# An expert loop whose TensorE text is laid out in another order: the 128-wide text moved ahead of the 144- and 160-wide ones

## What is computed

```python
D_MODEL, SEQ, N_EXPERTS, TOP_K, D_FF = 1024, 1024, 32, 4, 1024

top_vals, top_idx = lax.top_k(logits, TOP_K)
gates = jax.nn.softmax(top_vals, axis=-1)
# per expert e, on the tokens xb that chose it:
h = xb @ gu_w[e] + gu_b[e]                      # gu_w[e]: 1024 x 2048
x_glu = jnp.minimum(h[:, 0::2], SWIGLU_LIMIT)
x_lin = jnp.clip(h[:, 1::2], -SWIGLU_LIMIT, SWIGLU_LIMIT)
act = x_glu * jax.nn.sigmoid(SWIGLU_ALPHA * x_glu) * (x_lin + 1.0)
y = act @ dn_w[e] + dn_b[e]                     # dn_w[e]: 1024 x 1024
# y times its gate is added to the token's row
```

## Time and profile before

| | us |
|---|---|
| median of 3 runs | 2246.07 (2245.27 to 2248.84) |
| the profiled execution, own time | 2249.02 |
| its span in the trace | 2247.4 |
| TensorE matmuls busy | 2189.1 (97%) |
| TensorE weight loads busy (beside the matmuls) | 1594.6 (71%) |
| VectorE / ScalarE / GpSimd busy | 1283.0 / 472.6 / 344.5 |

### The profile page before, as it was taken

How to read it: one execution, slowest core, us unless ns; L and a number is a source line. 1 busy time by engine, 2 the same in 40 slices (tenths; PEclk the granted TensorE clock), 3 DMA queues, 4 the chain that set the end, 5 groups by cost and what they waited for, 6 DMA issues and landing times.

```text
span 2247.4 us, 49136 instructions
## 1 busy us (share of the span) xinstructions
PE 2189.1 (97%) x19188; PEld 1594.6 (71%) x19189; DVE 1283.0 (57%) x2529; ACT 472.6 (21%) x975; POOL 344.5 (15%) x356
## 2 busy tenths in 40 slices
PE   8999998899999999999999999999999999999997
PEld 3444444888545777887788877788778887788775
DVE  6566533455565455656555655566655665556664
ACT  3233001444423111111211111111111111111113
POOL 0000001122013212111121211122111221121211
PEclk9999999999999999999999999999999999999998
DMA  3111111332435868988888987799877998679987
GB/s 144 51 60 42 52 66 60 87 105 81 177 132 175 319 257 302 335 307 304 305 301 294 353 301 279 263 336 352 304 285 279 336 352 317 257 293 333 356 303 266
DMA packets 120367, 534.90 MB, mean 238 GB/s; under 512 B 27540, under 2 KB 61480, under 8 KB 87521
## 3 DMA queue, kind: packets, MB, share of 16 engines
q1 hardware_dynamic: 98416, 489.30, 56.5%
q0 software_dynamic: 21904, 44.98, 7.9%
HBM read 484.58 MB, written 40.05 MB: 233 GB/s over the span
## 4 chain that ended last, share of the span: by engine, by line
PE 95%; DMA 1%; issue 1%; DVE 1%; ACT 0%; SPq 0%; POOL 0%; another core or an unknown queue 0%; POOLq 0%; DVEq 0%; ACTq 0%
PE ps L2395 43%; PE ps L2441 17%; PE ps L1831 9%; PE ps L1929 5%; PE ps L2211 3%; PE ps L2425 2%; PE ps L2028 2%; PE ps L2476 2%; PE ps L1878 1%; PE ps L2037 1%; PE ps L2202 1%; PE ps L2010 1%; PE ps L2042 1%; PE ps L2130 1%; DMA arena<-sum_s 1%
## 5 line engine op out<-in xcount | busy, mean ns | idle before, releaser
L2395 PE MATMUL ps<-arena 128*128 128x128 f32 (+2 forms) x8192 | 986.4, 284 | 5.4 <-issue 3.7
L2395 PEld LDWEIGHTS ps<-arena 128*128 128x128 f32 x8192 | 978.2, 191 | 18.1 <-issue 16.1
L2441 PE MATMUL ps<-arena 128*64 128x512 f32 x1984 | 393.4, 543 | 2.4
L1685 DVE TENSOR_TENSOR arena<-arena 128x1024 f32<-128x1024 f32 x248 | 294.3, 1218 | 0.0
L2441 PEld LDWEIGHTS ps<-arena 128*64 128x64 f32 x1984 | 140.4, 137 | 207.2 <-issue 191.9
L1672 DVE TENSOR_SCALAR arena<-ps,arena 128x160 f32<-128x160 f32 x256 | 98.0, 383 | 306.1 <-PE ps L2395 304.0
L1086 ACT ACTIVATE arena<-arena 128x160 f32<-128x160 f32 x256 | 86.1, 336 | 802.9 <-DVE arena L1672 802.9
L1831 PE MATMUL ps<-arena 128*128 128x512 f32 x448 | 195.7, 594 | 0.0
L774 POOL DMA_INDIRECT sum_s<-arena,idx_s x31 | 51.5, 1660 | 841.2 <-ACT arena L1101 841.2
L1831 PEld LDWEIGHTS ps<-arena 128*128 128x128 f32 x448 | 84.7, 190 | 109.2 <-issue 109.2
L1929 PE MATMUL ps<-arena 128*128 128x512 f32 x280 | 120.6, 593 | 0.8 <-ACT arena L914 0.8
(11 more groups left out here) (292 smaller groups left out, 2141.7 us busy)
## 6 DMA issues: line engine op xcount, KB each, us to landing
arena<-gu_w SPq DMA_DIRECT2D x128, 2048.0 KB, 11.7
arena<-dn_w SPq DMA_DIRECT2D x128, 1024.0 KB, 13.9
arena<-dn_b SPq DMA_DIRECT2D x32, 512.0 KB, 15.3
arena<-w_in_t SPq DMA_DIRECT2D x26, 512.0 KB, 3.3
arena<-arena SPq DMA_DIRECT2D x50, 256.0 KB, 2.7
arena<-w_out SPq DMA_DIRECT2D x2, 2048.0 KB, 8.3
arena<-x SPq DMA_DIRECT2D x8, 512.0 KB, 3.5
xn_s<-arena SPq DMA_DIRECT2D x8, 512.0 KB, 2.6
```

The lines of the kernel that those rows point to most:

```text
L1685: nc.vector.tensor_tensor(dst[:, w, :], a[:, w, :], b[:, w, :], op).then_inc(s_ds, 1)
L2395: last = nc.tensor.matmul(ps[:, f % 2, k * C:k * C + size], wslot[u][:, kt, o:o + P], xT[:, kt, 0:size], start=kt == 0, stop=kt == KT - 1, ...
L2441: last = nc.tensor.matmul(ps[rows, bank, 0:width], acts[:, k, :], weights[:, k, :], start=first and k == 0, stop=k == K2 - 1, skip_group_c ...
```

## The change

In `gate_product` the condition is turned round, so that the 128-wide text is built first and the two wider ones with their shared steps second. The steps, their operands, widths and waits stay as they are. A 128-wide expert now runs into its text without a jump and jumps over the others at its end; a wider one jumps over the 128-wide text at its head and runs into the last steps without a jump.

```diff
             def gate_product(need, n, m):
-                with pe.If(need > 1):
+                with pe.If(need < 2):
+                    gate_up(n, m + 1, SIZES[0], range(0, END - SHARED))
+                with pe.Else():
                     with pe.If(need == 2):
                         gate_up(n, m + 1, SIZES[1], range(0, WIDE))
                     with pe.Else():
                         gate_up(n, m + 1, SIZES[2], range(0, WIDE))
                     gate_up(n, m + 1, C, range(WIDE, END - SHARED))
-                with pe.Else():
-                    gate_up(n, m + 1, SIZES[0], range(0, END - SHARED))
                 gate_up(n, m + 1, C, range(END - SHARED, END))
```

## The result

The change made the kernel slower, by very little: 2251.13 us median against 2247.17, 17 runs each, a ratio of 1.0017 with a 95% interval of 1.0010 to 1.0023, that is 2 to 5 us. The forecast was 2400 us; the number that came is that of rival 2, near the upper end of its working.

A forecast was written before the change was run, and what follows sets the result against it. TensorE was taken as the bound; 118 us for 31 back-jump misses plus 36 for wider passes' jumps made +154 on 2249.0, 2403 profiled, less 3 for 2400 us timed; whole range 2246 to 2500.

The forecast's parts named there:

- rival 2: Only the first pass differs: +1.4 us, from -1.2 to +5.1, giving 2247.5 to 2251 us; chance 0.32.
- What bounds the kernel: TensorE's matmuls fill 97% of the span; text order can change only how instructions reach it.
- The slot map and the text that stays: Counted loop slots: 1774 of 1792 in seven blocks, fetched once and kept; first-pass gaps fall at block starts.
- Steady passes at price 0: Later passes: moved jumps stay hidden, price 0; without cover under 9 us either way.
- Where the text stands: Jump target at slot 505 moved to 512, loop end spilling into block 8, refetches: +154 us, bounds 73 to 291.
- rival 1: Whole loop: text outgrows the eight blocks held, with refetches in later passes; 2400 us, range 2316 to 2500; chance 0.55.
- First pass: First expert's pass: jump misses added at the head, later gaps reduced or gone; sum +1.4 us, between -1.2 and +5.1.
- the second jump: First pass's head, slot 505 to 954 in block 4: a miss with no matmul queued, 5.2 us, bounds 2.61 and 8.9.
- The wait at slot 1024: First pass, after 35 pairs of matmuls: 0.4 us lost, instead of 1.56 us at slot 512.
- The 2.61 us: First pass, loss at the jump from slot 952 over the 128-wide text: gone, -2.61 us.
- Rival 3: First pass's head: both misses overlap the wait for the first xT copy; -4.2 us at most, 2242 us; chance 0.05.
- Rival 4: Skipped block 3 fetched late, at the first 144-wide expert (the fifth): one more miss, +2.6 us, 2253 us; chance 0.08.

The follow-up runs named there:

- b_k14: The kernel before with four more steps of its own in the 144- and 160-wide texts (WIDE = END - 14): 2248.81 us, ratio 1.0004.
- a_160_first: The kernel after with its two wider texts traded (128, 160, 144), so the first expert jumps once at the head: 2257.08 us, ratio 1.0035 against before.
- b_k13: The kernel before with five more own steps in the wider texts (WIDE = END - 13), last instruction on slot 1794: 2377.43 us, ratio 1.0548.
- both swapped runs: The text orders of before and after, each with experts 0 and 2 traded in the input arrays: ratios 1.0022 and 1.0048 against before.
- swap_after: The kernel after with experts 0 and 2 traded in the input arrays, so the first pass is 128 wide: 2259.63 us, ratio 1.0048 against before.
- b_pre: The kernel before with the alignment moved ahead of the first transposes, so TensorE enters the loop's first block earlier: 2247.77 us, ratio 0.9998.

## Why the prediction was wrong

- **What bounds the kernel**: held. TensorE from 800 to 2200 us is busy for 1397.68 us in both kernels, and only the first pass differs.
- **The slot map and the text that stays**: held, to the matmul: the gap moved from 27 to 18 pairs with the text. One reading of the map was wrong: block 3 is jumped over in the first pass, but it is read.
- **Steady passes at price 0**: held, 1394.42 us in both.
- **Where the text stands**: this is the step that failed. I let the forecast rest on the target at 505 being moved to the next block, which no row showed, and gave it 0.55. With targets on 1789 and 1791 nothing was moved (b_k14, ratio 1.0004, no packet later), and a_160_first shows two matmuls between 505 and the end of its block. The step from there to the loop's end was weak by itself: it called targets 13 and 11 slots short of a block the same position as one seven short. The loop's length is what counts, and the change doesn't alter it. The rest of rival 1 priced a state in which the kernel never was. There the sum came close (+123 us measured, 154 worked out), but partly by luck: it had a miss at each of 31 jumps back, where b_k13 shows 15, and no term for the clock, which makes 70.6 of 203.7 us in the profiled execution. Its bounds don't agree with its range either: 291 us would end at 2537, not 2500. The text said itself that it was a guess about something that the rows don't show; the weight beside it did not follow.
- **First pass**: the mechanism was right and one term too small. I took 5.2 us for the second jump, whose branch (line 2490) lasts 7.58 us in after's trace; the head gap grew from 1.77 to 9.69, 7.9 us. That lies under the bound of 8.9, but the bound proves nothing: its second part, 3.67, is the time of 27 matmuls, not of a fetch. What makes the gap is the wait for block 2 and then that for blocks 3 and 4 together. The wait at slot 1024, taken as 0.4, is not there. The 2.61 us are gone as worked out, and the 1.56 wholly. Sum: 7.9 - 1.56 - 2.61 = +3.7 us. The term that was missing is the clock: +2.1 us of matmuls at half clock behind a long gap. The profiled pair thus makes +5.8 us ahead of the second pass, the timed runs +2 to +5.
- **Rival 3**, the head hidden behind the tokens' copy: wrong by sign for after, though the copy is what before waits for there. **Rival 4**, block 3 read late in the fifth pass: not in this kernel (block 3 was read in the first pass, and no packet comes from 800 to 2200 us), but skipped blocks that are read later are what both swapped runs show.

## What to carry to other kernels

Where a loop's instructions just fit an engine's instruction memory, count their slots: the end of the loop is a cliff (four slots more: 5.5%), while the order of its texts only changes the first few passes, 2 to 11 us in the runs here. No rule for the order comes out of them: with the text that is run first right behind the branch (swap_after) the kernel was slower than with the other order, and with one jump less at the head (a_160_first) slower than after. Count the blocks that the first passes read, and what they cost in clock behind each gap. And when a forecast hangs on something that no row shows, it is a rival, not the forecast.

## What the runs showed of the hardware that was not expected

- Idle pieces of about 4 us or more were followed by half clock: 9.69 us of idle cost 2.1 us more, in the run with one jump less 9.9 us in two pieces cost 5.8. Of the shorter ones, 2.37 us in before and 2.69 in b_k14 were not, 2.93 in b_pre was, and so was 2.31 in swap_after, some 20 us behind one of 4.31. So several short gaps can cost more than one long one of the same sum, or less, by where they fall.
- A block that has been read is not always kept: after a first pass that left out one block, six packets came in in the second, and after one that left out two, eleven in the second and third.
- A spill of three slots (1792 to 1794) into the eighth block turned no instruction packets in 1400 us into 122. Where one 128-wide pass follows another, there were none even so.
